# A gate product moved ahead of the last input projection, and an attention's first scores moved ahead of TensorE's fence

## The chip, the cores and the metric

One core of a Trainium2 chip runs the whole program once. Its engines each work through a queue of their own, in order: TensorE (PE in the profile, with PEld for its weight loads), VectorE (DVE), ScalarE (ACT), GpSimd (POOL) and SyncE (SP), which here issues transfers. They meet only through semaphores. The metric is the device time of one execution in microseconds; less is better.

## The reference

Two transformer blocks in f32 on 512 tokens of width 1024. Only the first block's mixer matters here:

```python
h = rmsnorm(x, ln1[l])
proj = h @ w_in[l]
qkv_a, z_a, b_a, a_a, q_b, k_b, v_b = jnp.split(proj, IN_SPLITS, axis=-1)
y_a = gated_deltanet(qkv_a, z_a, b_a, a_a, conv_qkv[l], a_log[l], dt_bias[l], gdn_norm[l])
y_b = dilated_attention(heads_b(q_b), heads_b(k_b), heads_b(v_b), slopes)
x = x + jnp.concatenate([y_a, y_b], axis=-1) @ w_out[l]
```

`b_a` and `a_a` are four columns each: they become the gates of the delta rule (`beta` and the log-decay `g`, which is summed along each chunk of 64 tokens). All other parts of `proj` are multiples of 512 columns. The attention `y_b` has eight heads of 64 (four pairs of heads); its three dilations are computed as one softmax with a table of weights per distance.

## The kernel before, in words

**Input projections.** `proj` is made in seven products `w_in0` to `w_in6` of 512 columns each, and one narrow product `wba` of eight. A product of 512 columns has eight k-steps; each step has twelve matmuls (four output tiles, times three, since f32 is split into a high and a low half: hi*hi, hi*lo, lo*hi). ScalarE makes the high half of a weight tile (`hi_of`), VectorE the low half (`lo_of`), into a ring of four "units"; a unit is written again when TensorE has done the step that read it. While product n runs, ScalarE and VectorE take the finished tiles of product n-1 out of PSUM (`item`, at fixed k-steps): `w_in4` becomes `qb` and `w_in6` becomes `vb` on ScalarE, `w_in5` becomes `kb` on VectorE. The last product, `w_in6`, has no successor: its four tiles are copied by ScalarE after all its own units, just before the fence.

**The narrow product.** It comes after `w_in6`: 24 matmuls with weights of 8 columns (`narrow`, L2445 to L2447), a copy of the 8x512 result by VectorE (`narrow_out`, L1317), four transposes on TensorE (`narrow_rows`), and a copy of the transposed gates by VectorE (L1606).

**Fence 0.** Each engine drains, signals, and waits for the others' signals (`fence`). After it another layout of the memory is valid. VectorE's and ScalarE's work of the next stage starts behind it.

**The first attention.** It is one generator per engine, `attention("swa", ...)`, in 32 steps, and works on 20 units (a unit here is one half of a pair of heads in one of ten turns; it holds one or two pieces of up to 512 columns). In its step i, TensorE issues the scores of units i and i+1 if i is even (L2470), a filler of five matmuls (ten passes) at i = 7 (L2348), the transposes of the probabilities of unit i-7 ("P transposes", L2334, after GpSimd has scaled that unit) and, at odd i, the value products of units i-11 and i-10 (L2495). VectorE takes the minimum of unit i-1 (a fused add and reduction, L1412) and, at odd steps, the reciprocals of units i-5 and i-4 (L1418). ScalarE exponentiates unit i-3 and copies the P transposes of unit i-8. GpSimd scales units in order, each when its reciprocal is there (L2180). Scores share three PSUM banks, so the scores of a turn wait for minima of earlier units: those of units 4 and 5 for the minimum of unit 2, those of units 6 and 7 for that of unit 4.

**The gate front beside it.** A second generator per engine, `gdn_front`, is woven in by `run`. On VectorE it starts with the gates (L1618 on), waits for ScalarE's softplus (L1625), makes the decays for the gate sums and, later, takes those from PSUM (L1635, before the minimum of unit 4). On TensorE it holds the three matmuls of the gate sums (L2581 to L2583, body 4) and twelve groups of four transposes of q, k and v, called row transposes (0,0) to (3,2) below (L2334 again). VectorE copies and squares each q or k group (a "row block", L1645 to L1647), in its own bodies. At the end it computes norms from all of them (L1257 on, "the mean"), prepares factors, and reaches fence 1; TensorE runs another filler there.

**How `run` weaves.** In every turn it calls `next` once on the attention, then on the side generator as often as its pace says:

```python
n = turn - begins
for _ in range((n + 1) * num // den - n * num // den if n >= 0 else 0):
    if next(part, part) is part:
```

With `FRONT_PACE = (0, 3, 2)` (begins, num, den) that is 1, 2, 1, 2, ... calls. The first `next` of TensorE's `gdn_front` only reaches its first `yield`, and body k runs in call k+2. So the gate sums (body 4, call 6) come after attention step 3, and row transposes (0,0) (body 8, call 10) after step 6.

Of the kernel before, what the change touches and what calls it, by code (L numbers as in the profile page):

```python
# [84 lines left out]
class Signals:  # L85
# [13 lines left out]
    def up(self, name, *key, by=1):  # L99
        self.n[name] = self.n.get(name, 0) + by  # L100
        self.value[(name, *key)] = self.n[name]
        return self.sem(name), by

    def at(self, name, *key):
        return self.sem(name), 1 if self.counted is None else self.counted[0][(name, *key)]
# [351 lines left out]
def w8(r, n=512):  # L457
    return r[:, 0:8 * n].rearrange("p (k n) -> p k n", k=8)
# [89 lines left out]
class Plan:  # L548
# [3 lines left out]
    def __init__(self, m, I):  # L552
        self.chunks, self.ring, self.unit, self.step_of = {}, {}, {}, {}
        self.turn = 0
        for c in range(3):
            self.load(f"w_in{c}", I["w_in"][c], c)
        for c in range(3, 7):
            self.load(f"w_in{c}", I["w_in"][c], c % 3)
        for n in range(2):
            self.load(f"w_out{n}", I["w_out"][n], 1 + n)  # L560
        self.turn = 3
        for c in range(11):
            self.load(f"gu{c}", I["w_gu"][c])
            if c:
                self.load(f"ada{c - 1}", I["ada"][c - 1])
        for n in range(2):
            for i, kn in enumerate((8, 8, 6)):
                self.load(f"down{n}{i}", I["w_down"][3 * n + i][:, 0:kn * 512])
                if n == 0 and i:
                    self.load(f"ada{9 + i}", I["ada"][9 + i])  # L570
        for c in range(6):
            self.load(f"w2_{c}", I["w_in2"][c])
        for kv in range(2):
            self.load(f"cmp{kv}", I["cmp_w1"][kv])
        self.load("glu", I["glu"])
        self.load("ssm_wo", I["ssm_wo"])
        for c in range(2):
            self.turn = 2
            self.load(f"w2_{6 + c}", I["w_in2"][6 + c])
            self.load(f"w2_{8 + c}", I["w_in2"][8 + c])  # L580
            self.load(f"nsa_wo{c}", I["nsa_wo"][c])
        self.turn = 2
        for n in range(2):
            self.load(f"w_out2{n}", I["w_out2"][n])
        for i in range(NEXP):
            self.load(f"moe{i}", I["moe_gu"][i])
        r = lambda name: m.ring[self.ring[name][0]]
        for c in range(7):
            self.add(Chunk(f"w_in{c}", f"w_in{c}", w8(r(f"w_in{c}")), 8, "in", c in (3, 6)))
        self.narrow("wba", "in")  # L590
        for n in range(2):
            self.add(Chunk(f"w_out{n}", f"w_out{n}", w8(r(f"w_out{n}")), 8, "mid", True, m.yT))
        for c in range(11):
            self.add(Chunk(f"gu{c}", f"gu{c}", w8(r(f"gu{c}")), 8, "mid", False, lo="VG"))
        for n in range(2):
            for i, kn in enumerate((8, 8, 6)):
                w = r(f"down{n}{i}")[:, 0:kn * 512].rearrange("p (k n) -> p k n", k=kn)
                self.add(Chunk(f"down{n}{i}", f"down{n}{i}", w, kn, "mid", True, m.act[:, 8 * i:8 * i + kn, :],
                               (("gemm_dve", "act", 8 * i + kn - 1),), i == 0, i == 2, f"down{n}"))
        for c in range(6):  # L600
            self.add(Chunk(f"w2_{c}", f"w2_{c}", w8(r(f"w2_{c}")), 8, "mid", c == 4))
        self.narrow("wng", "mid")
        w = r("glu")[:, 0:2048].rearrange("p (k n) -> p k n", k=4)
        self.add(Chunk("glu", "glu", w, 4, "late", False, m.uT, (("merge_act", "gelu"),)))
        for c in range(2):
            self.add(Chunk(f"w2_{6 + c}", f"w2_{6 + c}", w8(r(f"w2_{6 + c}")), 8, "late", False))
            self.add(Chunk(f"w2_{8 + c}", f"w2_{8 + c}", w8(r(f"w2_{8 + c}")), 8, "late", False))
            self.add(Chunk(f"nsa_wo{c}", f"nsa_wo{c}", w8(r(f"nsa_wo{c}")), 8, "late", False, m.attT,
                           (("nsa_act", "T", 7),)))
            w = r("ssm_wo").rearrange("p (k n) -> p k n", k=4)[:, :, 512 * c:512 * c + 512]  # L610
            self.add(Chunk(f"ssm_wo{c}", "ssm_wo", w, 4, "late", False, m.ssT, (("gemm_dve", "glu", 3),)))
        for n in range(2):
            self.add(Chunk(f"w_out2{n}", f"w_out2{n}", w8(r(f"w_out2{n}")), 8, "late", True, m.mT))
# [69 lines left out]
def act_program(nc, m, s, p, I):  # L683
    a, at, up = nc.scalar, s.at, s.up
    K, C = m.K, m.C
# [74 lines left out]
    def narrow(name, n, w, part):  # L760
        u = p.unit[name]
        if u >= 4:
            a.wait_ge(*at("gemm_pe", *p.step_of[part, u - 4]))
        copy(m.units[part][:, u % 4, 0, 0:8 * n], w.rearrange("p k n -> p (k n)")).then_inc(*up("gemm_act", "nhi", name))
# [168 lines left out]
    a.dma_start(m.col[:, 80:], I["cols"][:, 80:]).then_inc(*up("dma_col", by=16))  # L933
    a.dma_start(m.cst[:, 256:], I["consts"][:, 256:]).then_inc(*up("dma_cst", by=16))
    for c, name in enumerate(WIN):
        if c:
            gemm(name, WIN[c - 1])
    a.wait_ge(*at("dma_col"))
    narrow("wba", 8, C["wba"], "in")
    for i in range(4):  # L940
        item("w_in6", i)
    fence(0)
# [61 lines left out]
    for c in range(8):  # L1004
        t, rows, other = c // 2, H64[c % 2], H64[1 - c % 2]
# [234 lines left out]
def dve_program(nc, m, s, p):  # L1240
# [67 lines left out]
    def narrow_lo(name, n, w, part):  # L1308
        u = p.unit[name] % 4
        U = m.units[part]  # L1310
        v.wait_ge(*at("gemm_act", "nhi", name))
        tt(U[:, u, 1, 0:8 * n], w.rearrange("p k n -> p (k n)"), U[:, u, 0, 0:8 * n].bitcast(F32),
           SUB).then_inc(*up("gemm_dve", "nlo", name))

    def narrow_out(name, n, tmp):
        v.wait_ge(*at("gemm_pe", "narrow", name))
        v.tensor_copy(tmp[0:n, :], s.bank("narrow", name)[0:n, :]).then_inc(*up("gemm_dve", "narrow", name))  # L1317
# [110 lines left out]
    def swa_table(h):  # L1428

        stt(table_of(h), K["ndist"], float(2.0 ** -(h + 1)), K["lnc"], MUL, ADD).then_inc(*up("swa_dve", "table", h))  # L1430
# [163 lines left out]
    for c, name in enumerate(WIN):  # L1594
        def between(k):
            if c == 3 and k == 0:
                v.wait_ge(*at("dma_cst"))
            if c >= 3 and k in (0, 6):
                swa_table(2 * c - 6 + k // 6)
        if c:  # L1600
            gemm(name, WIN[c - 1], between)
    v.wait_ge(*at("dma_col"))
    narrow_lo("wba", 8, C["wba"], "in")
    narrow_out("wba", 8, m.ba_tmp)
    v.wait_ge(*at("gemm_pe", "rows", "wba"))
    v.tensor_copy(m.bb[:, 0:32], s.bank("rows", "wba")[:, 0:32]).then_inc(*up("gemm_dve", "rows", "wba"))  # L1606
    fence(0)

    g = m.g
# [717 lines left out]
def pe_program(nc, m, s, p):  # L2327
# [16 lines left out]
    def fill(n, among=tuple(range(8))):  # L2344

        b = take(("fill", next(fill_at)), among=among)
        for _ in range(n):
            pe.matmul(b[:, 0:256], ones, m.cst[:, 0:256], start=True, stop=True)  # L2348

    def fence(i, filled=0):  # L2350
        pe.drain().then_inc(*up("fence_pe", i))
        if filled:
            fill(filled)
        pe.wait_ge(*at("fence_act", i))
        pe.wait_ge(*at("fence_dve", i))
        pe.wait_ge(*at("fence_pool", i))
# [93 lines left out]
    def narrow_rows(name, n, tmp):  # L2450
        b = take(("rows", name), (("gemm_act" if name == "wng" else "gemm_dve"), "rows", name))
        pe.wait_ge(*at("gemm_dve", "narrow", name))
        for t in range(4):
            ins = tp(b[:, n * t:n * t + n], tmp[0:n, 128 * t:128 * t + 128], n)
        ins.then_inc(*up("gemm_pe", "rows", name))
# [177 lines left out]
    pe.wait_ge(*at("dma_id"))  # L2633

    first_gemm("w_in0", "ln1", m.x0, False, "in")
    for name in WIN[1:]:
        gemm(name, ("ln1", "in"))
    narrow("wba", 8, ("ln1", "in"))
    narrow_rows("wba", 8, m.ba_tmp)
    fence(0)  # L2640

    run(attention("swa", SWA, swa_operands, m.swa_P, m.swa_T, (0, 1, 2), (3, 4), (5, 6)), (gdn_front(), FRONT_PACE))
    fence(1, 14)

    for t in range(4):
# [374 lines left out]
def run(main, *sides):  # L3020

    turn, live = 0, [(main, 0, 1, 1), *((part, *pace) for part, pace in sides)]
    while live:
        for thread in tuple(live):
            part, begins, num, den = thread
# [3 lines that stand above are left out]
                    live.remove(thread)  # L3029
                    break  # L3030
        turn += 1
# [196 lines left out]
```

## Time and profile before

| | us |
|---|---|
| median of 3 runs | 1705.51 (1703.37 to 1708.67) |
| the profiled execution | 1704.38 |
| its span, first to last instruction | 1703.1 |
| TensorE busy in the span | 1610.8 |
| VectorE, ScalarE, GpSimd busy | 933.4, 682.7, 345.3 |
| mean granted clock of TensorE | 0.983 |

A timeline row gives the start and the duration in us, the engine, the line, the operation with the tiles it writes and reads, a count, and in brackets the time that the engine sat idle before it with the operation that ended the wait. An end of a matmul is modelled: matmuls in a run start every 0.23 us though each is shown with 0.39. A table by windows gives each engine's busy time, and PEclk, the clock that TensorE was granted in that window (1.00 is 2.4 GHz, 0.50 is 1.2 GHz). The chain of waits goes back from the last instruction to whatever released it.

### The profile page before, as it was taken

How to read it: one execution, taken by the hardware profiler on the slowest of the kernel's cores; microseconds unless marked ns; L12 is line 12 of the kernel's file. 1: busy time of each engine (PE TensorE's matmuls, PEld its weight loads, DVE VectorE, ACT ScalarE, POOL GpSimd, SP SyncE). 2: the span in 40 equal slices, each digit the busy share in tenths (PEclk: the TensorE clock that was granted, in tenths of full speed). 3: DMA queues.
4: the chain of work that ended last, by engine and by line, in shares of the span. 5: the costliest groups of instructions: out<-in, count | busy, mean ns of one | idle time of the engine just before them, and what ended most of it. 6: DMA issues, size and time to landing. Idle time of an engine off the chain costs nothing.

```text
span 1703.1 us, 25065 instructions
## 1 busy us (share of the span) xinstructions
PE 1610.8 (95%) x9722; PEld 1175.6 (69%) x9722; DVE 933.4 (55%) x1883; ACT 682.7 (40%) x1469; POOL 345.3 (20%) x356
## 2 busy tenths in 40 slices
PE   6999889899999999999998899989999988999995
PEld 5888579778888888877887666668887853343332
DVE  4753565555766665673536878843537642232336
ACT  3432663554333334554425666643434521121112
POOL 0000454002222210000001455500101133333320
PEclk9999899999999999999998999999999989999998
DMA  6331000331444444324200000053124579999964
GB/s 260 130 113 52 1 2 3 120 141 68 191 192 193 198 185 161 136 99 149 100 25 1 2 9 8 8 198 131 50 99 173 223 269 381 382 399 388 381 240 160
DMA packets 41829, 256.21 MB, mean 150 GB/s; under 512 B 18411, under 2 KB 18539, under 8 KB 25201
## 3 DMA queue, kind: packets, MB, share of 16 engines
q1 hardware_dynamic: 24848, 231.88, 34.8%
q0 software_dynamic: 13600, 11.34, 2.2%
q10 hardware_dynamic: 3264, 11.40, 1.8%
q8 instruction: 79, 1.29, 0.3%
q14 instruction: 38, 0.30, 0.1%
HBM read 294.51 MB, written 22.02 MB: 186 GB/s over the span
## 4 chain that ended last, share of the span: by engine, by line
PE 82%; DVE 7%; DMA 5%; ACT 2%; issue 2%; POOL 1%; SPq 1%; ACTq 0%; POOLq 0%; DVEq 0%
PE banks L2406 17%; PE banks L2407 17%; PE banks L2408 17%; PE banks L2922 8%; PE banks L2334 5%; PE banks L2938 4%; DMA plain<-in_moe_gu,arena 3%; PE banks L2470 2%; PE banks L2495 2%; PE banks L2604 2%; POOL plain L2180 1%; PE banks L2348 1%; PE banks L2771 1%; DVE units L1293 1%; PE banks L2799 1%
## 5 line engine op out<-in xcount | busy, mean ns | idle before, releaser
L689 ACT ACTIVATE units<-arena 128x512 fp32r<-128x512 f32 (+2 forms) x416 | 250.7, 626 | 446.8 <-PE banks L2408 440.2
L1293 DVE TENSOR_TENSOR units<-arena,units 128x512 fp32r<-128x512 f32 x370 | 252.2, 705 | 305.8 <-ACT units L689 305.3
L2406 PE MATMUL banks<-hx,units 128*128 128x512 f32 x800 | 313.9, 392 | 3.7 <-DVE hx L1823 1.8
L2407 PE MATMUL banks<-hx,units 128*128 128x512 f32 x800 | 312.3, 390 | 0.0
L2408 PE MATMUL banks<-hx,units 128*128 128x512 f32 x800 | 312.3, 390 | 0.0
L2406 PEld LDWEIGHTS banks<-hx,units 128*128 128x128 f32 x800 | 150.8, 188 | 35.6 <-issue 4.5
L2408 PEld LDWEIGHTS banks<-hx,units 128*128 128x128 f32 x800 | 150.7, 188 | 31.4
L2407 PEld LDWEIGHTS banks<-hx,units 128*128 128x128 f32 x800 | 150.8, 188 | 30.8
L689 ACT ACTIVATE arena<-banks 128x512 f32<-128x512 f32 (+3 forms) x171 | 93.4, 563 | 154.6 <-PE banks L2334 55.8
L2406 PE MATMUL banks<-units 128*128 128x512 f32 x380 | 148.6, 391 | 4.2 <-DVE units L1293 4.2
L2408 PE MATMUL banks<-units 128*128 128x512 f32 x380 | 148.0, 389 | 0.0
L2407 PE MATMUL banks<-units 128*128 128x512 f32 x380 | 147.9, 389 | 0.0
L2334 PE MATMUL banks<-arena 128*128 128x128 f32 (+4 forms) x680 | 97.3, 278 | 26.4 <-ACT arena L689 15.4
L2334 PEld LDWEIGHTS banks<-arena 128*128 128x128 f32 (+4 forms) x680 | 74.5, 143 | 66.3 <-issue 42.9
L2922 PE MATMUL banks<-arena,plain 128*64 128x512 f32 x512 | 114.2, 598 | 1.8 <-issue 1.8
L2170 POOL TENSOR_TENSOR units<-arena,units 128x512 fp32r<-128x512 f32 x44 | 62.5, 1422 | 236.4 <-ACT units L689 236.4
L2922 PEld LDWEIGHTS banks<-arena,plain 128*64 128x64 f32 x512 | 37.1, 139 | 75.2 <-issue 75.2
L2406 PEld LDWEIGHTS banks<-units 128*128 128x128 f32 x380 | 71.3, 188 | 21.1 <-DVE units L1293 3.6
L2408 PEld LDWEIGHTS banks<-units 128*128 128x128 f32 x380 | 71.3, 188 | 15.0
L2407 PEld LDWEIGHTS banks<-units 128*128 128x128 f32 x380 | 71.3, 188 | 14.6
L689 ACT ACTIVATE plain<-banks 128x512 f32<-128x512 f32 (+2 forms) x92 | 50.5, 549 | 65.6 <-PE banks L2604 15.7
L1765 DVE CUSTOM_DVE_ANT_0 arena<-arena 128x1024 f32<-128x1024 f32 x48 | 73.7, 1549 | 0.0
(440 smaller groups left out, 2490.6 us busy)
## 6 DMA issues: line engine op xcount, KB each, us to landing
arena<-in_moe_gu SPq DMA_DIRECT2D x32, 2048.0 KB
arena<-in_w_in SPq DMA_DIRECT2D x17, 2048.0 KB
arena<-in_moe_dn SPq DMA_DIRECT2D x32, 1024.0 KB, 9.0
arena<-in_ada SPq DMA_DIRECT2D x12, 2048.0 KB
arena<-in_w_gu SPq DMA_DIRECT2D x11, 2048.0 KB
arena<-in_w_out SPq DMA_DIRECT2D x4, 2048.0 KB
arena<-in_w_down SPq DMA_DIRECT2D x4, 2048.0 KB
arena<-in_cmp_w SPq DMA_DIRECT2D x2, 2048.0 KB
```

Of the source, the lines that this page charges most:

```text
L689: return func(dst, src, ACT.Copy, scale=scale)
L1293: tt(lo, src, hi.bitcast(F32), SUB).then_inc(*up("gemm_dve", "lo", c.part, u))
L1765: v.tensor_tensor_reduce(w, w, m.crow, 1.0, 0.0, MUL, ADD, m.mod[:, f:f + 1]).then_inc(*up("gemm_dve", "ada", c, i))
L2170: tt(U[:, u % 4, 1, :], c.w[:, k, :], U[:, u % 4, 0, :].bitcast(F32), SUB).then_inc(*up("gemm_pool", "lo", c.part, u))
L2334: return pe.transpose(o, i, ident[0:rows, 0:rows])
L2406: pe.matmul(bs[i], sh[:, q], mh, start=c.first and k == 0, stop=False)
L2407: pe.matmul(bs[i], sh[:, q], ml, start=False, stop=False)
L2408: return pe.matmul(bs[i], sl[:, q], mh, start=False, stop=c.last and k == c.kn - 1)
L2470: ins = pe.matmul(bs[half][:, piece.col:piece.col + piece.n], q[rows, H4[piece.tile]], k[rows, 0:piece.n], start=True, stop=True)
L2495: ins = pe.matmul(ob[rows, H4[t]], values[half](r), T[(j - 1 + half) % 4][:, piece.col + 128 * r:piece.col + 128 * r + 128], start=fresh a ...
L2922: ins = pe.matmul(b[rows, :], xT[:, k, rows], w[half][:, k % w[half].shape[1], :], start=k == 0, stop=k == last)
L2938: ins = pe.matmul(b[rows, :], aT[:, k, rows], wd[half][:, k, n * 512:(n + 1) * 512], start=k == 0, stop=k == 1)
```

## The change

Three engines get the narrow product one place earlier, between `w_in5` and `w_in6`; its transposes come within `w_in6` (before k-step 4), and VectorE's two copies behind k-steps 3 and 7. On TensorE the attention's first step (the scores of units 0 and 1) moves between the fence's signal and its waits, behind two new waits for the last `qb` and `kb` tiles; `run` then gets the rest of the attention, and TensorE's front with begin -1.

```diff
         for c in range(7):
+            if c == 6:
+                self.narrow("wba", "in")
             self.add(Chunk(f"w_in{c}", ...
-        self.narrow("wba", "in")
@@ ScalarE
     for c, name in enumerate(WIN):
+        if c == 6:
+            a.wait_ge(*at("dma_col"))
+            narrow("wba", 8, C["wba"], "in")
         if c:
             gemm(name, WIN[c - 1])
-    a.wait_ge(*at("dma_col"))
-    narrow("wba", 8, C["wba"], "in")
     for i in range(4):
         item("w_in6", i)
     fence(0)
@@ VectorE
+            if c == 6 and k == 3:
+                narrow_out("wba", 8, m.ba_tmp)
+            if c == 6 and k == 7:
+                v.wait_ge(*at("gemm_pe", "rows", "wba"))
+                v.tensor_copy(m.bb[:, 0:32], s.bank("rows", "wba")[:, 0:32]).then_inc(*up("gemm_dve", "rows", "wba"))
+        if c == 6:
+            v.wait_ge(*at("dma_col"))
+            narrow_lo("wba", 8, C["wba"], "in")
         if c:
             gemm(name, WIN[c - 1], between)
@@ TensorE
-    def fence(i, filled=0):
+    def fence(i, filled=0, first=None):
         pe.drain().then_inc(*up("fence_pe", i))
         if filled:
             fill(filled)
+        if first:
+            first()
         pe.wait_ge(*at("fence_act", i))
...
-    for name in WIN[1:]:
+    for name in WIN[1:6]:
         gemm(name, ("ln1", "in"))
     narrow("wba", 8, ("ln1", "in"))
-    narrow_rows("wba", 8, m.ba_tmp)
-    fence(0)
-
-    run(attention("swa", SWA, swa_operands, m.swa_P, m.swa_T, (0, 1, 2), (3, 4), (5, 6)), (gdn_front(), FRONT_PACE))
+
+    def ahead(k):
+        if k == 4:
+            narrow_rows("wba", 8, m.ba_tmp)
+    gemm("w_in6", ("ln1", "in"), ahead)
+
+    swa = attention("swa", SWA, swa_operands, m.swa_P, m.swa_T, (0, 1, 2), (3, 4), (5, 6))
+    pe.wait_ge(*at("gemm_act", "qb", 3))
+    pe.wait_ge(*at("gemm_dve", "kb", 3))
+
+    def first_turn():
+        next(swa)
+    fence(0, first=first_turn)
+
+    run(swa, (gdn_front(), (-1, *FRONT_PACE[1:])))
     fence(1, 14)
```

## Rows read from the trace of the kernel before

**Rows 1.** The page, part 4: shares of the chain of waits by engine.

```profile
PE 82%; DVE 7%; DMA 5%; ACT 2%; issue 2%; POOL 1%; SPq 1%; ACTq 0%; POOLq 0%; DVEq 0%
```

**Rows 2.** Timelines of PE, ACT and DVE before fence 0 and just behind.

```profile
173.93 0.39 PE L2445 MATMUL banks<-hx,units 128*8 128x512 f32 x1
...
174.13 2.07 ACT L689 ACTIVATE arena<-banks 128x512 f32<-128x512 f32 x4 [7.84 <-PE banks L2408]
...
179.24 0.39 PE L2447 MATMUL banks<-hx,units 128*8 128x512 f32 x1
...
180.91 0.19 DVE L1606 COPY arena<-banks 128x32 f32<-128x32 f32 x1 [0.56 <-PE banks L2334]
...
181.40 0.18 DVE L1618 TENSOR_TENSOR arena<-arena 128x16 f32<-128x16 f32 x1 [0.30 <-DVE arena L1606]
```

**Rows 3.** Timelines of DVE and PE, 185 to 193 us: the gate front.

```profile
185.31 0.18 DVE L1625 TENSOR_TENSOR arena<-arena 128x16 f32<-128x16 f32 x1 [1.35 <-ACT arena L954]
...
186.26 0.58 PE L2581 MATMUL banks<-arena 128*128 128x16 f32 x2 [1.71 <-DVE arena L1630]
...
187.13 0.08 DVE L1412 DVE_READ_ACCUMULATOR2_ANT plain<- 128x1 f32 x1
...
187.75 0.18 DVE L1635 COPY arena<-banks 128x16 f32<-128x16 f32 x1
...
188.47 0.18 DVE L1639 TENSOR_SCALAR arena<-arena 128x16 f32<-128x16 f32 x1
189.76 0.29 DVE L1412 CUSTOM_DVE_ANT_0 arena<-banks,arena 128x128 f32<-128x128 f32 x1 [1.11 <-PE banks L2470]
...
190.45 0.08 DVE L1412 DVE_READ_ACCUMULATOR2_ANT plain<- 128x1 f32 x1
...
190.68 2.08 PE L2470 MATMUL banks<-arena 64*128 64x256 f32 x8 [0.95 <-DVE plain L1418]
```

**Rows 4.** Windows: length, busy time by engine, then PEclk, DMA share, GB/s.

```profile
185.50:186.00 0.50, 0.00 (x0) 0.00 (x0) 0.44 (x3) 0.50 (x1) 0.00 (x0) 0.50 0.00 0
...
195.50:196.00 0.50, 0.50 (x4) 0.39 (x3) 0.47 (x2) 0.00 (x0) 0.50 (x2) 0.80 0.00 0
```

**Rows 5.** Timelines of PE and DVE, 193 to 200 us.

```profile
193.59 3.37 PE L2348 MATMUL banks<-arena 128*128 128x256 f32 x10
193.84 0.69 DVE L1645 COPY plain<-banks 128x512 f32<-128x512 f32 x1 [0.23 <-PE banks L2334]
...
199.11 0.17 DVE L1418 RECIPROCAL plain<-plain 128x4 f32<-128x4 f32 x1
```

**Rows 6.** Groups by line to 280 us: busy us, mean ns, idle before.

```profile
L1412 DVE CUSTOM_DVE_ANT_0 plain<-banks,arena 128x256 f32<-128x256 f32 (+3 forms) x26 | 11.4, 480 | 5.2 <-PE banks L2470 5.2
```

**Rows 7.** Timeline of POOL, 186 to 246 us.

```profile
199.38 3.62 POOL L2180 TENSOR_SCALAR arena<-arena,plain 128x128 f32<-128x128 f32 x4 [1.82 <-DVE plain L1418]
203.28 10.78 POOL L2180 TENSOR_SCALAR plain<-plain 128x256 f32<-128x256 f32 x10 [0.28 <-DVE plain L1418]
214.04 3.10 POOL L2180 TENSOR_SCALAR arena<-arena,plain 128x512 f32<-128x512 f32 x2
217.12 11.06 POOL L2180 TENSOR_SCALAR plain<-plain 128x128 f32<-128x128 f32 x10
```

**Rows 8.** Timelines of PE and DVE, 226 to 239 us: the end.

```profile
226.79 0.63 PE L2334 MATMUL banks<-arena,plain 128*128 128x128 f32 x4 [0.48 <-POOL plain L2180]
...
228.87 0.60 PE L2334 MATMUL banks<-arena 128*128 128x128 f32 x4
229.40 1.09 PE L2495 MATMUL banks<-plain,arena 128*64 128x128 f32 x16
...
229.51 0.69 DVE L1645 COPY plain<-banks 128x512 f32<-128x512 f32 x1 [0.93 <-PE banks L2334]
...
231.68 0.18 DVE L1257 TENSOR_SCALAR arena<-arena 128x32 f32<-128x32 f32 x1
...
238.93 4.58 PE L2334 MATMUL banks<-arena 128*128 128x128 f32 x40 [0.40 <-issue]
```

More of the change, by code:

```diff
@@ L1599, in between @@
                 swa_table(2 * c - 6 + k // 6)
+            if c == 6 and k == 3:
[6 more added lines that the diff above has]
+            narrow_lo("wba", 8, C["wba"], "in")
         if c:
             gemm(name, WIN[c - 1], between)
[L1602 to L1606, printed above, removed]
     fence(0)
```

## The prediction

> **What bounds the kernel now.** First the page's chain: TensorE carries 82% of it [rows 1], so an edit near a fence counts only where the stage behind it starts or ends at another time. Then the timelines around fence 0. TensorE runs the narrow product from 173.93 to the end of its last slot, 179.24 + 0.23 = 179.47; the four evictions of `w_in6` (174.13 to 176.20 on ScalarE) lie beside it. Behind it come a copy, four small transposes and a second copy, which ends at 181.10; VectorE's first operation of the gate front starts at 181.40, 1.93 us after the slot [rows 2]. From there the stage hangs on hand-overs: ScalarE's softplus (VectorE waits 1.35 us for it), the gate sums, scores of units 4 and 5, scores of units 6 and 7 [rows 3]. TensorE waits in between, and its clock is at half from 185.5 at the latest until 195.7 (0.80 over the half microsecond from 195.5) [rows 4]. Behind that GpSimd decides: it idled 1.82 us before unit 4 for VectorE's reciprocal, and from 203.28 to 228.18 it never stops [rows 7]. At the very end it is VectorE: fence 1 opens for TensorE at 238.93, after 0.40 us in which TensorE's filler was already done [rows 8].
>
> **The change, step by step** (d: new start less old start).
>
> *What costs nothing.* The narrow product stays the same 24 matmuls, 5.54 us, inside the stream. Its operands and the first copy fall where each k-step of twelve matmuls (2.7 us) leaves ScalarE and VectorE idle most of the time, and the unit ring runs three steps ahead; without that cover each would cost its own length. The added waits on `qb` and `kb` are for copies made while the last projection still runs; behind them in TensorE's queue stand the drain and the first scores. Those scores now run under the evictions, but after their minima VectorE waits for softplus as before [rows 3]: nothing gained on the chain.
>
> *Step A, the start.* What goes is the tail of 1.93; what is late next are the evictions, which have lost their cover. The stream ends 0.4 later than 179.47 for the four small transposes now within it (eight columns each; four of 128 columns take 0.60 [rows 8], so 0.2 to 0.6): 179.87. The evictions start 0.20 after that, as 174.13 against 173.93, and take 2.07: 182.14. VectorE follows 0.30 later, as 181.40 follows 181.10: 182.44. d = +1.04; with the lower bound of the transposes and half the hand-over +0.7, and +1.5 if the stream stumbles where it is broken. I take +1.0.
>
> *Step B, the gate sums change places.* `run` gets TensorE's front with begin -1 after a turn already consumed, so the single quota of turn 0 is never given: each piece of that front comes one `next` late, while ScalarE and VectorE keep their pace. The gate sums, after step 3 until now, come after step 4, behind the scores of units 4 and 5; and VectorE needs the sums before it turns to unit 4. Unit 2's minimum ends at 187.21 + 1.0 = 188.21; scores start 0.15 later (190.53 to 190.68), take 2.08; sums 1.49 (186.26 to 187.75): 191.93. VectorE's five operations take 0.90 (to 188.65), and unit 4's minimum starts at 192.83 for 189.76 [rows 3]. d = +3.07, or +1.3 if scores and sums ran at the full clock in half the time.
>
> *Step C, the first row transposes.* They stood right behind the scores of units 6 and 7; VectorE copied them from 193.84 [rows 5]. Now the filler's ten passes and the first P transposes come before them. The scores start 0.92 after unit 4's minimum, as before, at 193.75, and end at 195.83. The old filler (3.37 from 193.59, the clock back at 195.7) gives 0.46 for a slow pass and 0.23 for a fast one. The clock had come back 5.0 after 190.68, where unbroken work began; I put it at 198.8: 6.5 slow passes and 3.5 fast, to 199.6. With 0.53 for P transposes (four of the same size hold TensorE from 228.87 to 229.40) and 0.64 until VectorE has row transposes (228.87 to 229.51) [rows 8] it starts at 200.8; bounds 199.3 and 202.6 by the clock. A row block takes it 2.17 (229.51 to 231.68) and the minima of units 7 and 8 are three pieces of 0.48 [rows 6]: the reciprocal for units 4 and 5 comes at 204.4 for 199.11, and GpSimd's unit 4 0.27 later at 204.6 for 199.38. d = +5.2 (+3.7 to +7.0). VectorE's next round, 2.17 + 1.44, lets GpSimd start unit 6 at 208.2 for 203.28: d = +5.0.
>
> *Step D, the loop through GpSimd.* From step 13 on a row block's transposes stand behind P transposes that wait for GpSimd, and behind value products. Unit 6 done at 208.2 + 1.81 = 210.0; 0.53 + 1.03 (value products, 1.09 from 229.40 with the overlap of the next) + 0.64: 212.2; VectorE's 2.17 + 1.44 and 0.27: GpSimd's unit 10 at 216.1. It would be free at 208.2 + 3.62 + 3.10 = 214.9 [rows 7], so 1.2 idle where it had none; with the shorter minima of these units 0.9. I take 1.0: d = +6.0. The later reciprocals come in time by the same count.
>
> *Step E, the end.* Row transposes (3,0) stood ahead of unit 18's wait for GpSimd and now come behind it and a value product: 226.79 + 6.0 + 0.53 + 1.03 + 0.64 = 235.0; two row blocks of 2.17, and the mean starts at 239.4 for 231.68 [rows 8]. d = +7.7. VectorE's whole tail hangs on it, while TensorE's filler moves by some 6 and covers none of it. Behind fence 1 nothing changes.
>
> Sum 1.0 + 2.1 + 1.9 + 1.0 + 1.7 = **+7.7 us**. On the profiled execution (span 1703.1, in all 1704.38) that is 1712.1; this execution lies 1.1 under the median of the runs, 1705.51, which would give 1713.2. I forecast 1712.5. With the bounds of A and C the sum is +5.9 to +10.0, so 1710 to 1715.
>
> **Rule against row.** The clock stood at 0.50 in the half microsecond from 185.5 [rows 4], after a stretch in which TensorE had only two pairs of scores and four small transposes. The Trainium skill, "TensorE: Matmul & The Clock Gate", Part 1 (the HAM clock gate), says that the throttled state is the default and that sustained activity releases it. By that rule the empty stretches that the change leaves behind the fence cannot help, and the sum stays at +7.7 or goes to its upper end; the trace agrees as to the fall.
>
> **Rivals.** *The clock holds* (0.13). With one pair of scores ahead, TensorE stays at 2.4 GHz through the hand-overs. Then B is +1.3 in all, the filler 2.3, GpSimd's unit 4 starts at 200.4 and unit 6, behind two units of 1.81, at 204.0: +0.75; with D and E as before +3.4: 1708. For it: the work before the fence is longer. Against it: the scores of units 2 and 3 then stand alone between some 181 and 188, emptier than what let the clock fall.
>
> *The lag is absorbed* (0.19): no slower than can be told. The place is GpSimd's start of unit 4, where it idled 1.82, and VectorE's waits for TensorE of 1.11 and 0.93 [rows 3, 8]. If the late front falls into these, A alone is left, price +1.0: 1706.5. It holds from the point where the reciprocal for units 4 and 5 comes before 200.1. Against it: step B alone moves VectorE by more than all its waits on that way.
>
> *It gives what its words promise* (0.06). The tail of 1.93 is hidden and the evictions cost nothing, VectorE starting from its own last copy: -1.5, near 1704. Against it: VectorE's fence waits for ScalarE's signal, which follows the last eviction.
>
> *Worse* (0.07). The idle of step D returns at each of three row blocks and the clock comes back late: +11, 1716.5.
>
> **From cases to numbers.** The forecast has 0.55. About 0.3% (5.1 us) is what a measurement of this kernel tells from no change. The forecast lies some 2 beyond that; I count nine tenths of it as slower (0.50), with *worse* 0.07: slower 0.57. Same: its rest, the clock, the absorbed lag and most of the hidden tail, 0.40. Faster 0.03, since all that the edited stretch holds is some 3 us. The forecast's own range is 1710 to 1715; 1705 to 1716 takes in the clock and the absorbed lag.
>
> **What would show it.** VectorE's first front operation 1 us later; the gate sums behind a pair of scores, VectorE idle near 3 us before its copy of them; the first row transposes behind the filler; GpSimd idle near 4 us before unit 4 and about 1 before unit 10; the mean at the stage's end 7 to 8 later. I am wrong if GpSimd's unit 6 starts less than 2 us later than 203.28, if the clock stays at full, or if the stage's end moves less than GpSimd does.

## The result, and the profile after

The changed kernel takes 1715.49 us (median of 7 runs, 1713.66 to 1718.27), the kernel before 1705.51 (7 runs on the same chip); the ratio is 1.0054, 95% interval 1.0039 to 1.0069, that is +6.7 to +11.8 us. The profiled execution took 1715.49 us with a span of 1714.2. It is slower, 3 us beyond the forecast of 1712.5.

Two executions don't start the stage at the same time of their own span, so I measure a stage length: from the first matmul of the stream's last two slots ahead of fence 0 (the last projection and the narrow product, in either order) to TensorE's first transposes behind fence 1. Of before it runs from this row to the last row of [rows 8], 238.93 - 152.17 = 86.76 us.

```profile
152.17 0.39 PE L2406 MATMUL banks<-units,hx 128*128 128x512 f32 x1
```

After the change it is 247.03 - 151.07 = 95.96: **+9.20 us**. All starts of after below have to be raised by 152.17 - 151.07 = 1.10 to stand beside those of before; I call that aligned.

The start of the stage, timelines of PE, ACT and DVE after (start, us, engine, line, tile, count, idle before and its releaser); they answer to [rows 2].

```profile
151.07 0.39 PE L2452 MATMUL banks<-hx,units 128*8 128x512 f32 x1
...
179.15 2.07 ACT L690 ACTIVATE arena<-banks 128x512 f32<-128x512 f32 x4 [10.84 <-PE banks L2415]
179.36 1.14 PE L2477 MATMUL banks<-arena 64*128 64x128 f32 x8 [0.25 <-issue]
...
181.34 0.18 DVE L1623 TENSOR_TENSOR arena<-arena 128x16 f32<-128x16 f32 x1 [12.20 <-ACTq L693]
```

The scores do run ahead, at 179.36. VectorE, though, now waits for ScalarE's queue (`ACTq`), behind the four evictions, and starts at 182.44 aligned for 181.40.

The gate front of after, PE and DVE, and behind it the first row transposes' copy; they answer to [rows 3, 5].

```profile
187.29 2.08 PE L2477 MATMUL banks<-arena 64*128 64x128 f32 x8 [2.71 <-DVE plain L1414]
189.30 0.61 PE L2588 MATMUL banks<-arena 128*128 128x16 f32 x2
...
190.82 0.17 DVE L1640 COPY arena<-banks 128x16 f32<-128x16 f32 x1 [3.07 <-PE banks L2590]
...
191.62 0.28 DVE L1414 CUSTOM_DVE_ANT_0 arena<-banks,arena 128x128 f32<-128x128 f32 x1
...
192.53 2.08 PE L2477 MATMUL banks<-arena 64*128 64x256 f32 x8 [1.75 <-DVE plain L1420]
...
194.54 3.62 PE L2353 MATMUL banks<-arena 128*128 128x256 f32 x10
...
199.07 0.69 DVE L1650 COPY plain<-banks 128x512 f32<-128x512 f32 x1 [3.60 <-PE banks L2339]
...
202.42 0.17 DVE L1420 RECIPROCAL plain<-plain 128x4 f32<-128x4 f32 x1
```

The sums at 189.30 stand behind a pair of scores, and VectorE sits idle for 3.07 us before their copy; for the rows' copy it waits 3.60 us, behind filler and P transposes, where it waited 0.23 before.

GpSimd after, which answers to [rows 7]:

```profile
202.69 4.12 POOL L2185 TENSOR_SCALAR arena<-arena,plain 128x128 f32<-128x128 f32 x4 [3.29 <-DVE plain L1420]
206.79 6.70 POOL L2185 TENSOR_SCALAR plain<-plain 128x256 f32<-128x256 f32 x6
215.75 3.62 POOL L2185 TENSOR_SCALAR plain<-plain 128x128 f32<-128x128 f32 x4 [2.26 <-DVE plain L1420]
219.72 3.10 POOL L2185 TENSOR_SCALAR arena<-arena,plain 128x512 f32<-128x512 f32 x2 [0.35 <-DVE plain L1420]
...
227.89 6.70 POOL L2185 TENSOR_SCALAR plain<-plain 128x256 f32<-128x256 f32 x6 [1.48 <-DVE plain L1420]
```

It waits for VectorE's reciprocal 3.29 us at the first row block (1.82 before), and then 2.26, 0.35 and 1.48 us where it had never stopped. Its last unit ends at 234.59, 7.5 us later than 228.18 when aligned.

The end of the stage, DVE and PE, which answers to [rows 8]:

```profile
224.96 0.69 DVE L1650 COPY plain<-banks 128x512 f32<-128x512 f32 x1 [2.64 <-PE banks L2339]
...
236.13 0.69 DVE L1650 COPY plain<-banks 128x512 f32<-128x512 f32 x1 [5.53 <-PE banks L2339]
...
240.35 0.18 DVE L1259 TENSOR_SCALAR arena<-arena 128x32 f32<-128x32 f32 x1
...
247.03 4.57 PE L2339 MATMUL banks<-arena 128*128 128x128 f32 x40 [0.86 <-issue]
```

The mean starts at 241.45 aligned, 9.77 later than 231.68. TensorE's clock is at half earlier and for longer than in [rows 4]: windows of after (length, busy time of PE, PEld, DVE, ACT, POOL, then PEclk, DMA share, GB/s).

```profile
183.00:183.50 0.50, 0.50 (x3) 0.19 (x4) 0.44 (x2) 0.46 (x4) 0.00 (x0) 0.84 0.00 0
183.50:184.00 0.50, 0.50 (x4) 0.00 (x0) 0.00 (x0) 0.48 (x2) 0.00 (x0) 0.50 0.00 0
...
196.50:197.00 0.50, 0.50 (x3) 0.41 (x2) 0.00 (x0) 0.00 (x0) 0.50 (x1) 0.51 0.00 0
197.00:197.50 0.50, 0.50 (x4) 0.45 (x3) 0.00 (x0) 0.00 (x0) 0.50 (x1) 1.00 0.00 0
```

That is 13.6 us at 1.2 GHz (from about 183.4 to 197.0) where before had 10.2 (185.5 to 195.7).

### The profile page after: what moved, and what is told of

Same layout as the page of the kernel before. It is cut to its first block, busy times and chain, and to the rows that moved or that the text cites. A ratio compares the mean times of both kernels' runs of the same rounds, so it can differ in the third digit from the quotient of the medians.

```text
span 1714.2 us, 25066 instructions
## 1 busy us (share of the span) xinstructions
PE 1614.7 (94%) x9722; PEld 1176.2 (69%) x9722; DVE 932.3 (54%) x1883; ACT 683.1 (40%) x1469; POOL 344.6 (20%) x356
## 4 chain that ended last, share of the span: by engine, by line
PE 82%; DVE 7%; DMA 5%; ACT 3%; issue 2%; SPq 1%; POOL 0%; ACTq 0%; DVEq 0%; POOLq 0%
PE banks L2413 17%; PE banks L2415 17%; PE banks L2414 17%; PE banks L2940 7%; PE banks L2339 6%; PE banks L2956 4%; DMA plain<-in_moe_gu,arena 3%; PE banks L2502 2%; PE banks L2477 2%; PE banks L2611 2%; PE banks L2353 1%; PE banks L2789 1%; ACT arena L690 1%; DVE units L1295 1%; PE banks L2817 1%
## 5 line engine op out<-in xcount | busy, mean ns | idle before, releaser
L690 ACT ACTIVATE units<-arena 128x512 fp32r<-128x512 f32 (+1 forms) x416 | 250.7, 626 | 450.3 <-PE banks L2415 438.5
## 6 DMA issues: line engine op xcount, KB each, us to landing
arena<-in_moe_gu SPq DMA_DIRECT2D x32, 2048.0 KB, 10.2
```

What stands on the lines that cost most here:

```text
L690: return func(dst, src, ACT.Copy, scale=scale)
```

## The experiments

| kernel | stage from | to | stage | against before | at half clock | total, ratio to before |
|---|---|---|---|---|---|---|
| before | 152.17 | 238.93 | 86.76 | | 10.2 | |
| changed | 151.07 | 247.03 | 95.96 | +9.20 | 13.6 | 1.0054 [1.0039, 1.0069] |
| e1_pace | 152.14 | 239.44 | 87.30 | +0.54 | 10.2 | 1.0003 [0.9987, 1.0018] |
| e2_lag_only | 150.89 | 246.12 | 95.23 | +8.47 | 10.2 | 1.0040 [1.0025, 1.0054] |
| e3_narrow_only | 151.99 | 238.87 | 86.88 | +0.12 | 6.8 | 1.0002 [0.9992, 1.0011] |
| e4_sums_back | 151.43 | 244.87 | 93.44 | +6.68 | 10.2 | single run |
| e5_rows_back | 151.73 | 241.51 | 89.78 | +3.02 | 13.6 | single run |
| e6_late_vb | 151.21 | 236.26 | 85.05 | -1.71 | 6.8 | 0.9992 [0.9977, 1.0006] |
| e7_late_vb_fill | 151.22 | 233.65 | 82.43 | -4.33 | 0 | 0.9972 [0.9962, 0.9983] |
| e8_after_fill | 151.29 | 246.53 | 95.24 | +8.48 | 6.8 | single run |
| e9_before_fill | 151.71 | 235.25 | 83.54 | -3.22 | 0 | 0.9980 [0.9969, 0.9991] |
| e10_after_fill3 | 152.03 | 245.54 | 93.51 | +6.75 | 0 | single run |

All but the ratios are in us. The stage comes from one profiled execution each. "At half clock" is how long TensorE was granted 1.2 GHz in it, read from windows of 0.5 us. Since the clock falls at different places even behind the same work (last section), two stages that differ in this column differ by a part of the clock too. The totals of single runs are not read: runs of the kernel before itself lie between 1702.1 and 1712.6 us.

**Is it the lag? e1_pace** gives the front's quota of turn 0 back.

```diff
     def first_turn():
         next(swa)
+        next(front)
+    front = gdn_front()
     fence(0, first=first_turn)
-    run(swa, (gdn_front(), (-1, *FRONT_PACE[1:])))
+    run(swa, (front, (-1, *FRONT_PACE[1:])))
```

> The stage is measured from the first matmul of the stream's last two slots ahead of the fence to the first matmul behind the next fence: 86.76 us before, 95.96 us after (+9.20). This kernel is the changed one with the gate front's first quota given back: the early part takes its step as well, so the front stands at every turn where it stood before. Theory (the front's lag is the cost, and all that follows to the stage's end comes from it): the stage is 87.8 us, only the +1.04 of the four evictions that the fence now waits for is left; the total is about 1 us above before. Rival 1 (the evictions' delay grows by itself through the attention's turns, the lag is no cause): the stage stays at 94 to 96 us. Rival 2 (TensorE's clock is late by the changed order): +4 us or more, with the granted clock at half beyond 196 us.

Measured 87.30 us, +0.54, half a microsecond under the theory: nearly all is gone, and the total cannot be told from before. GpSimd waits only at the first row block, as before it did ([rows 7] has the 0.28 too):

```profile
199.89 3.63 POOL L2185 TENSOR_SCALAR arena<-arena,plain 128x128 f32<-128x128 f32 x4 [1.33 <-DVE plain L1420]
203.80 10.78 POOL L2185 TENSOR_SCALAR plain<-plain 128x256 f32<-128x256 f32 x10 [0.28 <-DVE plain L1420]
214.56 3.11 POOL L2185 TENSOR_SCALAR arena<-arena,plain 128x512 f32<-128x512 f32 x2
```

**e2_lag_only** puts the lag alone into the kernel before.

```diff
     fence(0)
 
-    run(attention("swa", ...), (gdn_front(), FRONT_PACE))
+    swa = attention("swa", ...)
+    next(swa)
+    run(swa, (gdn_front(), (-1, *FRONT_PACE[1:])))
```

> The kernel before, with the lag alone: its projections stand in the old order and nothing is issued ahead of the fence's wait, but the attention's first turn takes no step of the gate front. Theory (the lag is the cost): the stage of 86.76 us grows by 7.5 to 8.5 us, that is the +9.2 without the evictions' 1.04; the total is about 8 us above before. Rival 1 (the evictions are the cause): at most +1 us. Rival 2 (the clock): about +3 us, the half-clock stretch being as much longer.

Measured +8.47 us of stage, 1.0040 in total. The waits of GpSimd are those of the changed kernel to 0.02 us behind the first row block:

```profile
201.78 4.12 POOL L2180 TENSOR_SCALAR arena<-arena,plain 128x128 f32<-128x128 f32 x4 [3.78 <-DVE plain L1418]
...
214.83 3.62 POOL L2180 TENSOR_SCALAR plain<-plain 128x128 f32<-128x128 f32 x4 [2.26 <-DVE plain L1418]
218.80 3.10 POOL L2180 TENSOR_SCALAR arena<-arena,plain 128x512 f32<-128x512 f32 x2 [0.34 <-DVE plain L1418]
...
226.97 6.70 POOL L2180 TENSOR_SCALAR plain<-plain 128x256 f32<-128x256 f32 x6 [1.47 <-DVE plain L1418]
```

Taking the lag out removes the loss, putting it alone in brings it: the narrow product's new place is not the cause.

**e3_narrow_only** has that new place with an ordinary fence and an ordinary `run`.

```diff
-    swa = attention("swa", ...)
-    pe.wait_ge(*at("gemm_act", "qb", 3))
-    pe.wait_ge(*at("gemm_dve", "kb", 3))
-    def first_turn():
-        next(swa)
-    fence(0, first=first_turn)
-    run(swa, (gdn_front(), (-1, *FRONT_PACE[1:])))
+    fence(0)
+    run(attention("swa", ...), (gdn_front(), FRONT_PACE))
```

> The narrow product ahead of the last input projection alone: an ordinary fence, and the attention's first turn and the front as before. Theory (lag): the evictions of the last projection are exposed, +1.0 us to the stage (87.8 us), and nothing grows from it; the total is about 1 us above before. Rival 1 (the evictions' delay grows in the turns): +5 to +9 us. A third way, the early scores being what cost: no more than +1 us here, and the whole +9 with the front's quota given back.

Measured +0.12 where the theory said +1.0. The delay is there at the start (first scores at 182.40 aligned for 181.25, +1.15) and gone by GpSimd's unit 4 (199.50 for 199.38). In between the clock falls only at 188.5 here, and is at half for 6.8 us instead of 10.2:

```profile
188.00:188.50 0.50, 0.29 (x4) 0.32 (x6) 0.50 (x3) 0.50 (x3) 0.00 (x0) 1.00 0.00 0
188.50:189.00 0.50, 0.50 (x6) 0.35 (x5) 0.47 (x5) 0.50 (x4) 0.00 (x0) 0.55 0.06 16
195.00:195.50 0.50, 0.50 (x3) 0.38 (x3) 0.50 (x1) 0.00 (x0) 0.50 (x1) 0.62 0.00 0
```

So the later clock gave the delay back in this execution (the scores of units 4 and 5 took 1.80 us for 2.08, the filler 3.10 for 3.37); that it does so in each is not shown.

**Which half of the lag? e4_sums_back and e5_rows_back** keep the lag and advance by one body of the front only the gate sums, or only the row transposes.

```diff
 # e4_sums_back
-            if i == 4:
+            if i == 3:
 # e5_rows_back
-            if i in GDN_TURN:
-                t, n = GDN_TURN[i]
+            if i + 1 in GDN_TURN:
+                t, n = GDN_TURN[i + 1]
```

> The changed kernel with its lag kept, except that the two gate-sum matmuls come one body of the front earlier, so that they stand ahead of the scores of units 4 and 5 again; the row transposes stay a turn late. Tells which half of the lag costs. Theory (the rows' turn feeds the later idle of GpSimd, the sums only shift its start): the stage (86.76 us before, 95.96 after) is 93.3 to 94.3 us, +6.5 to +7.5, and GpSimd still waits some 3, 2.3, 0.3 and 1.5 us ahead of units 4, 10 and the two later ones. Rival (the late sums are the root, the rest follows from them): 87.8 to 88.8 us, +1 to +2, and GpSimd's later waits are gone.

> The changed kernel with its lag kept, except that each transpose of the gate rows comes one body of the front earlier, so that the rows stand where they stood before; the gate sums stay behind the scores of units 4 and 5. Theory (late sums cost their +2.96 at unit 4's minimum, and nothing grows from it once the rows are in time): the stage is 89.3 to 90.3 us, +2.5 to +3.5, with no wait of GpSimd over 0.3 us ahead of unit 10 and later. Rival (only the rows matter, the sums' delay is taken up): 86.8 to 88 us. Second rival (the sums are the root): 93 to 96 us, the waits stay.

Measured +6.68 and +3.02, both within what the theory gave. With e1 (both in time) and the changed kernel (both late) this is a square: late rows cost 95.96 - 89.78 = 6.18 us with late sums and 93.44 - 87.30 = 6.14 without; late sums cost 2.52 and 2.48. In these executions the two add and do not feed each other. The rows' 6.1 is taken between stages with the same time at half clock (13.6 in both, 10.2 in both). The sums' 2.5 is not: each time the stage with late sums has 3.4 us more at half clock, so how much of the 2.5 is the place of the sums and how much the clock stays open. In e2, with both late and 10.2 us at half, the stage is 8.47 longer; with e1's 0.54 that makes 9.01 of the 9.20 and leaves some 0.2 for the longer half clock, which speaks for the place. GpSimd in e4 keeps the later waits (first fence), in e5 there are none (second). The third has a clock row of e4 and then one of e5.

```profile
213.57 3.63 POOL L2185 TENSOR_SCALAR plain<-plain 128x128 f32<-128x128 f32 x4 [2.25 <-DVE plain L1420]
217.55 3.11 POOL L2185 TENSOR_SCALAR arena<-arena,plain 128x512 f32<-128x512 f32 x2 [0.34 <-DVE plain L1420]
...
225.72 6.71 POOL L2185 TENSOR_SCALAR plain<-plain 128x256 f32<-128x256 f32 x6 [1.46 <-DVE plain L1420]
```

```profile
201.95 3.63 POOL L2185 TENSOR_SCALAR arena<-arena,plain 128x128 f32<-128x128 f32 x4 [1.86 <-DVE plain L1420]
205.86 10.79 POOL L2185 TENSOR_SCALAR plain<-plain 128x256 f32<-128x256 f32 x10 [0.27 <-DVE plain L1420]
216.63 3.10 POOL L2185 TENSOR_SCALAR arena<-arena,plain 128x512 f32<-128x512 f32 x2
```

```profile
194.00:196.00 2.00, 2.00 (x11) 1.74 (x10) 0.00 (x0) 0.00 (x0) 2.00 (x2) 0.96 0.00 0
...
196.00:198.00 2.00, 2.00 (x7) 1.65 (x6) 1.74 (x5) 0.00 (x0) 2.00 (x2) 0.50 0.00 0
```

**How much is the clock? e8_after_fill** adds 5 and 6 filler matmuls to the changed kernel, **e10_after_fill3** 4 more behind the gate sums.

```diff
-FILL = {"swa": {7: 5}, "nsa": {}}
+FILL = {"swa": {3: 6, 7: 5}, "nsa": {}}          # e10: {3: 6, 5: 4, 7: 5}
...
     def first_turn():
         next(swa)
+        fill(5, (7,))
```

> The changed kernel with its lag kept, and with filler matmuls in TensorE's idle behind the first scores (5 fillers) and behind the second (6), whose products nothing reads. It asks how much of the +9.20 is the clock, granted at half from 183.7 to 197 us. If the clock stays at full: the attention's scores and the filler run in half their time there, and the theory (the lag's order of work costs, the clock adds about 3.4) gives a stage of 92 to 93 us, +5.2 to +6.2. Rival 1 (the clock is the whole cost): 87 to 88 us. Rival 2 (the clock is beside the path): 95 to 97 us with the granted clock at full. Should the clock fall all the same, it says nothing on this.

> The changed kernel with its lag, the 5 and 6 fillers of the earlier version, which held the clock until 190.7 us only, and 4 more behind the gate sums (idle 2.2 us). It asks what the +9.20 is without the clock's part. Theory (the order of work costs, the clock adds about 3.4): with the clock at full through 198 us the stage is 92 to 93 us. Rival 1 (the clock is the whole cost): 87 to 88 us. Rival 2 (clock beside the path): 95 us, as with the 5 and 6. The waits of GpSimd ahead of units 10 and later (2.26, 0.34, 1.48 us) stay under the theory, since they come from the lag, after the clock is back in any case.

In e8 the clock fell all the same, later: 0.55 from 190.5, half until 197, and 0.72 us of stage are won; so, as expected for that case, it does not answer the question. In e10 it stays at full:

```profile
188.00:192.00 4.00, 2.65 (x18) 1.98 (x19) 2.40 (x17) 3.34 (x14) 0.00 (x0) 1.00 0.01 2
192.00:196.00 4.00, 4.00 (x22) 3.03 (x21) 1.39 (x9) 2.00 (x9) 3.90 (x5) 1.00 0.00 0
```

The stage is 93.51, 2.45 us less than the changed kernel's, and 0.5 above what the theory gave. The 2.45 is at least what this kernel's stage loses to the clock; it is not a share of the +9.20: the kernel before stands at half clock too, and is 3.22 us shorter without it (e9 below). With the clock at full in both, the changed order is 93.51 - 83.54 = 9.97 us longer; so the order of work makes the rise, or nearly all of it, without the clock. GpSimd waits 2.25, 0.34 and 1.46 us behind the first row block as in the changed kernel, so those waits are not the clock's. The added fillers hold something up themselves: they waited 1.09 us for ScalarE and ended into the scores of units 6 and 7, which start 41.14 us into the stage (39.90 in e8). Without that 1.24, e10 would be near 92.3, inside the expected 92 to 93, and the 9.97 near 8.7: estimates from these rows that no run tests.

**What can be had? e6_late_vb** is e1 with ScalarE's four evictions behind the fence, in its front's bodies 7 to 10; **e7_late_vb_fill** adds 2 and 3 fillers to it; **e9_before_fill** puts 2 and 3 fillers into the kernel before, with no other change.

```diff
 # e6_late_vb, over e1_pace (ScalarE)
-    for i in range(4):
-        item("w_in6", i)
     fence(0)
...
+            if 7 <= i < 11:
+                item("w_in6", i - 7)
 # e7_late_vb_fill, over e6_late_vb (TensorE)
-FILL = {"swa": {7: 5}, "nsa": {}}
+FILL = {"swa": {3: 3, 7: 5}, "nsa": {}}
...
     def first_turn():
         next(swa)
+        fill(2, (7,))
 # e9_before_fill, over before (TensorE)
-FILL = {"swa": {7: 5}, "nsa": {}}
+FILL = {"swa": {1: 2, 3: 3, 7: 5}, "nsa": {}}
...
```

> The changed kernel with the front's quota given back, and ScalarE's four evictions of the last projection moved behind the fence, into its own front's bodies 7 to 10, so that the fence waits for none of them. Theory (the evictions at the fence are the +1.04 that is left when the lag is gone): the stage is 85.3 to 86.3 us, 0.5 to 1.5 below before, of which 0.4 is the early scores' share. Rival (the fence's wait is bound by something else, or ScalarE is what the front then waits for): 87.8 us or more.

> The version without the lag and with ScalarE's four evictions behind the fence (its stage was 85.05 us, 1.71 below before), and with filler matmuls in TensorE's two idle stretches there, 2 fillers behind the first scores (idle 1.03 us) and 3 behind the second (idle 1.38 us), to keep the clock up. If the clock is granted in full through 186 to 194 us, where it was 0.57: the three score blocks of 2.08 us there and the 4.00 us of the last filler halve, of which by the chain about 2 to 3 us reach the stage's end: 82 to 83 us, the total 4 to 5 us under before. Rival (what the scores gain, VectorE's and GpSimd's chain takes back): 84.5 to 85 us. If the fillers are too few: the clock falls all the same, 85 us.

> The kernel before with nothing of the change, and with filler matmuls in its two idle stretches, 2 behind the first scores (idle 1.03 us) and 3 behind the second (idle 1.71 us). It asks whether the gain of the version without the lag (stage 82.43 us against 86.76) needs the changed order at all. Theory (the fillers' share is the clock's, and is there in the old order too; they took 85.05 to 82.43, that is 2.62): the stage is 83.6 to 84.6 us, total 2 to 3 us under before. Rival (without the earlier start of the attention and with the old tail ahead of the fence the fillers do not hold the clock): 86 to 87 us, the clock at half for some 10 us as before.

e6 gives -1.71 us, 0.25 beyond the theory's range, and a total whose interval holds 1; with 6.8 us at half clock for 10.2 in e1 and before, part of the 1.71 can be the clock's. e7 gives -4.33 and 0.9972 in total, e9 -3.22 (0.06 beyond its range) and 0.9980: both beat the kernel before. Most of e7's gain is therefore there in the old order too. In e7 the clock is at full throughout, the old filler takes 2.32 us, and GpSimd does not stop even at the first row block:

```profile
188.94 2.32 PE L2353 MATMUL banks<-arena 128*128 128x256 f32 x10
```

```profile
194.25 3.91 POOL L2185 TENSOR_SCALAR arena<-arena,plain 128x128 f32<-128x128 f32 x4
198.14 10.66 POOL L2185 TENSOR_SCALAR plain<-plain 128x256 f32<-128x256 f32 x10
```

Between e7 and e9 the totals' intervals overlap; that the changed order (early scores, narrow product in the stream) is worth the 1.11 us by which their stages differ is not shown.

## Why the prediction was right, and where its sizes were off

The direction and the mechanism held: a stage that starts 1 us later, and a lag of TensorE's front that first GpSimd and then the stage's end pay for. 1715.49 lies within the wide range, 0.5 above the forecast's own range of 1710 to 1715. The sum was +7.7; the stage gave +9.20. In the sum's own terms, with E taken at the stage's end, A to E measured 1.04, 1.92, 1.65, 2.90 and 1.69, for 1.0, 2.1, 1.9, 1.0 and 1.7. (The profiled executions differ by 11.1: the stage of after starts 1.1 earlier, and the code behind it, which is the same, takes 3.0 longer. After has a stretch of 6.8 us at half clock near 333 us that before lacks; that this makes the 3.0 is not shown.) Of the signs that I named, VectorE waits 3.07 before the sums as said; GpSimd idles 3.29 for near 4 and 2.26 for about 1, and the mean moves by 9.8 for 7 to 8.

*Step A* said +1.0 at VectorE's first operation, and it was +1.04. Two terms of it were off against each other: the stream ended 0.18 later than I said, with the transposes at the upper end of my bounds, and the hand-over was 0.12 (179.15 + 2.07 to 181.34) instead of 0.30. How much reaches the end is less sure than the sum took it: 0.54 in e1, 0.12 in e3, 0.73 as the difference of the changed kernel and e2; only e1 has the same time at half clock as what it is held against.

*Step B*: unit 4's minimum at 192.72 aligned, against 192.83. The late sums cost 2.5 us at the stage's end (e4, e5), some of it perhaps the clock's, against 2.07 in the sum.

*Step C*: right in kind, a little over: the row copy at 200.17 aligned against 200.8, GpSimd's unit 4 at 203.79 against 204.6 and unit 6 at 207.89 against 208.2. The filler took 3.62, less than my six and a half slow passes gave.

*Step D* is the term that was mis-sized: the idle before unit 10 is 2.26, not 1.0, and "the later reciprocals come in time by the same count" is wrong, 0.35 and 1.48 follow. I let TensorE start its P transposes as soon as GpSimd was done with unit 6 (206.79 + 1.81 = 208.60). PE's rows of after show what I had left out:

```profile
208.39 0.66 PE L2339 MATMUL banks<-arena 128*128 128x128 f32 x4
209.82 0.66 PE L2339 MATMUL banks<-arena,plain 128*128 128x128 f32 x4 [0.77 <-ACT plain L690]
...
211.44 0.66 PE L2339 MATMUL banks<-arena 128*128 128x128 f32 x4
```

They start at 209.82, 1.22 us later than I let them, and the idle exceeds my number by 1.26. TensorE was itself busy until 209.05, with unit 5's P transposes (the first row), and then stood idle for 0.77, which ScalarE's copy ended: the P transposes have two banks in the kernel, and a copy has to free one first. ScalarE's rows show why it came late:

```profile
207.44 1.14 ACT L690 ACTIVATE arena<-banks,arena 128x128 f32<-128x128 f32 x4 [2.43 <-PE banks L2339]
...
209.16 0.61 ACT L690 ACTIVATE plain<-banks 128x512 f32<-128x512 f32 x1
```

The copy at 209.16 is that of unit 4's P transposes, which TensorE had done at 205.79. In ScalarE's queue, which kept its pace, the copy of the late row transposes of v (207.44) stands ahead of it, and waited 2.43 us for TensorE. So the lag came back into TensorE by way of ScalarE, an engine that my step D did not have. The same wait returns in later turns (1.05 us at 222.66, 0.70 at 226.06, 1.28 at 233.81). GpSimd's end moves by 7.5 us where step D had it at 6.0. This part of the rival *worse*, to which I gave 0.07, came true.

*Step E*: 9.77 - 7.5 = 2.3 from GpSimd to the mean, against 1.7. The mean then stands at +9.8 rather than +7.7, and VectorE's tail of it took 0.57 less (247.03 - 240.35 against 238.93 - 231.68), hence +9.20. That step E's 1.7 holds at the stage's end is luck: two errors cancel.

Of the rivals, *the clock holds* would have come out higher than its price: with the clock at full the stage is still +6.75 (e10), against +3.4. Its price kept D at 1.0; in e10 D is 2.9 as in the changed kernel (GpSimd's last unit ends 5.06 later, its unit 6 starts 2.15 later). It put that start at +0.75; of the 2.15, 1.24 is what I estimate the added fillers to hold up. *The lag is absorbed* and *what its words promise* fall with the result itself, and e2 brings the loss back with the lag alone. The rule of the Trainium skill that I weighed ("TensorE: Matmul & The Clock Gate", Part 1, the HAM clock gate) left the sum at +7.7 or towards its upper end, +10.0. The longer half clock, 13.6 us for 10.2, agrees with it. That the stage came out at +9.20 is not its doing: e2 has +8.47 with 10.2 us at half, as before, and what took the sum up is step D.

## What to carry to other kernels

Where one step of an interleaved pair of work streams is taken out of the loop to run early, give the partner its step as well, or check every place where the partner's order against it changes: here a missing quota, not the moved work, was 8.5 of 9.2 us. When a delay enters a loop through several engines, walk it for each turn and include the buffers that must come free and every engine that frees them; here the wait that one turn showed came back in three later ones. Before reordering around a hand-over where TensorE stands idle, look at the granted clock: here 5 fillers in two idle stretches took 3.2 us off the stage by themselves, more than the best order without them (1.7 in e6).

## What was not expected of the hardware

The clock falls at different places behind the same work. In the kernel before and in e2, TensorE has the same rows up to the end of the second scores, with the same idle stretches between them (0.86, 0.38 and 1.03 us). These scores stand here in before, then in e2, with a window of e2 behind them:

```profile
183.42 1.13 PE L2470 MATMUL banks<-arena 64*128 64x512 f32 x4 [1.03 <-DVE plain L1412]
...
182.14 1.13 PE L2470 MATMUL banks<-arena 64*128 64x512 f32 x4 [1.03 <-DVE plain L1412]
...
184.00:186.00 2.00, 0.00 (x0) 0.00 (x0) 1.83 (x9) 1.97 (x5) 0.00 (x0) 1.00 0.00 0
```

Before, the clock fell at 185.5, 2.1 us after the start of these scores, and stood at half for 10.2 us. In e2 TensorE then stood idle until 186.08 with 2.4 GHz granted, and the clock fell at 186.3, 4.2 us after their start. In e3 it fell at 188.5, for 6.8 us, behind idle stretches of 1.07 and 1.56 us like those of before (1.03 and 1.71), though with an idle of 2.19 us ahead of the first scores. The Trainium skill, "TensorE: Matmul & The Clock Gate", Part 1 (the HAM clock gate), says that the window in which the chip judges TensorE's activity runs freely, not from the kernel's start; a fall that comes at another place behind the same work fits that. No kernel here has two profiled executions, so how often one kernel meets which fall is not known.

Fillers of 1.13 and 1.56 us in the idle stretches behind the first and the second scores were enough to keep 2.4 GHz in e7 and e9; in e8, 2.43 and 2.86 us held it there, and in the next idle stretch, of 1.75 us, it fell.
